# Gathers of half rows into both halves of the partitions, and down matrices laid out as 16 KB per partition

## The reference, cut to what matters

```python
    def expert_block(args):
        xb, e = args
        hmid = jax.nn.silu(xb @ w_gate[e]) * (xb @ w_up[e])   # (rows, 1024) x (1024, 512), twice
        return hmid @ w_down[e]                               # (rows, 512) x (512, 1024)
```

## Time and profile before

| | |
|---|---|
| median of 3 runs | 1599.68 us |
| the profiled execution | 1603.98 us |
| its span | 1601.9 us |
| PE busy | 1300.0 us (81%) |
| DVE / ACT / POOL busy | 395.9 / 202.2 / 205.9 us |
| mean granted TensorE clock | 0.943 of full |
| DMA traffic | 471.18 MB, mean 294 GB/s |

### The profile page before, as it was taken

How to read it: one execution, slowest core, us unless ns; L and a number is a source line. 1 busy time by engine, 2 the same in 40 slices (tenths; PEclk the granted TensorE clock), 3 DMA queues, 4 the chain that set the end, 5 groups by cost and what they waited for, 6 DMA issues and landing times.

```text
span 1601.9 us, 19565 instructions
## 1 busy us (share of the span) xinstructions
PE 1300.0 (81%) x8158; PEld 884.9 (55%) x8158; DVE 395.9 (25%) x809; ACT 202.2 (13%) x318; POOL 205.9 (13%) x228
## 2 busy tenths in 40 slices
PE   8999998999777787778369999799887787777850
PEld 7888876565444444444158887656444444444420
DVE  1211214431111111111145663443111111111116
ACT  1000011000000000000044652200000000000002
POOL 0000001122111111111010000112211111111104
PEclk8999998899999999999779999889999999999985
DMA  9922204799999999999793202469999999999954
GB/s 236 303 105 105 106 1 167 257 399 403 404 409 409 399 410 405 410 399 407 240 293 150 82 29 102 163 252 375 403 406 397 406 412 392 412 395 401 417 182 119
DMA packets 109162, 471.18 MB, mean 294 GB/s; under 512 B 14391, under 2 KB 49207, under 8 KB 91684
## 3 DMA queue, kind: packets, MB, share of 16 engines
q1 hardware_dynamic: 93324, 443.09, 72.2%
q0 software_dynamic: 10240, 17.06, 3.2%
q10 hardware_dynamic: 5552, 10.39, 2.3%
HBM read 459.53 MB, written 19.19 MB: 299 GB/s over the span
## 4 chain that ended last, share of the span: by engine, by line
PE 40%; DMA 29%; SPq 24%; DVE 3%; issue 2%; POOL 1%; ACT 1%; POOLq 0%; DVEq 0%; ACTq 0%
SPq L357 23%; PE ps L547 18%; DMA ring<-in_moe_w_gate 14%; PE ps L785 8%; PE ps L631 7%; DMA ring<-in_moe_w_up 6%; DMA ring<-in_moe_w_down 4%; PE ps L804 4%; DMA Bt<-yrows 1%; DMA ring<-yrows 1%; DMA ring<-in_a_w_in 1%; PE ps L775 1%; PE ps L649 1%; PE ps L683 1%; PE ps L571 1%
## 5 line engine op out<-in xcount | busy, mean ns | idle before, releaser
L785 PE MATMUL ps<-ring,A 128*64 128x256 f32 x4096 | 487.5, 393 | 144.7 <-DMA ring<-in_moe_w_up 97.2
L785 PEld LDWEIGHTS ps<-ring,A 128*64 128x64 f32 x4096 | 320.4, 142 | 332.8 <-issue 135.6
L547 PE MATMUL ps<-A,ring 128*128 128x260 f32 x1280 | 286.2, 386 | 2.5 <-DMA ring<-in_a_w_in 2.5
L804 PE MATMUL ps<-ring,C 128*64 128x512 f32 x1024 | 239.1, 609 | 40.1 <-DMA ring<-in_moe_w_down 15.8
L547 PEld LDWEIGHTS ps<-A,ring 128*128 128x128 f32 x1280 | 245.6, 192 | 41.0 <-issue 2.7
L1396 DVE TENSOR_TENSOR C<-C,ps 128x256 f32<-128x256 f32 x64 | 26.9, 420 | 769.9 <-ACT C L1017 769.9
L804 PEld LDWEIGHTS ps<-ring,C 128*64 128x64 f32 x1024 | 79.1, 139 | 159.3 <-issue 137.7
L484 POOL DMA_INDIRECT A<-x,idx x64 | 61.2, 957 | 487.1 <-PE ps L775 458.3
L631 PE MATMUL ps<-Bt,ring 128*128 128x260 f32 x512 | 116.1, 385 | 1.0 <-ACT C L942 0.8
L631 PEld LDWEIGHTS ps<-Bt,ring 128*128 128x128 f32 x512 | 96.1, 190 | 20.1 <-DVE A L1244 2.5
L1017 ACT ACTIVATE C<-ps 128x256 f32<-128x256 f32 x64 | 24.6, 384 | 569.3 <-PE ps L785 569.2
(11 more groups left out here) (210 smaller groups left out, 662.2 us busy)
## 6 DMA issues: line engine op xcount, KB each, us to landing
ring<-in_moe_w_gate SPq DMA_DIRECT2D x64, 2048.0 KB
ring<-in_moe_w_up SPq DMA_DIRECT2D x64, 2048.0 KB
ring<-in_moe_w_down SPq DMA_DIRECT2D x64, 2048.0 KB
ring<-in_a_w_in SPq DMA_DIRECT2D x24, 512.0 KB, 17.8
ring<-in_b_w_in SPq DMA_DIRECT2D x8, 1024.0 KB
ring<-yrows SPq DMA_DIRECT2D x8, 832.0 KB
x<-C ACTq DMA_DIRECT2D x10, 416.0 KB
ring<-in_a_w_out SPq DMA_DIRECT2D x2, 2048.0 KB
```

The costliest lines, as they stand in the source:

```text
L547: mm = pe.matmul(bank, lhs(k), rhs(k), start=(k == 0), stop=(k == KT - 1))
L785: mm = pe.matmul(ps[hf * ROWS:(hf + 1) * ROWS, 1, u * FH:(u + 1) * FH], xgT[:, k, :], ring[:, slot, col:col + FH], start=(k == 0), stop=(k ...
L804: mm = pe.matmul(ps[nh * ROWS:(nh + 1) * ROWS, 2, :], hidT[:, at:at + ROWS], ring[:, slot, m * D + nh * 512:m * D + (nh + 1) * 512], start ...
```

## The change

Four things are done.

1. The down matrices are laid out as `(p m)`: partition p holds rows 4p to 4p+3, one piece of 16 KB in DRAM. The DMA has the same bytes and the same destination slot.
2. `turn_hidden` has to give partition p the hidden values 4p to 4p+3. Two transposes become four pairs of 64 by 64 products with the identity (partitions 0 to 63 onto 0 to 63, and 64 to 127 onto 64 to 127), and one product of the whole identity with four of its columns stands ahead of them.
3. A token's row is gathered as two half rows of 2 KB by two indirect DMAs: the first half to partitions 0 to 47, the second half to partitions 64 to 111. `turn_rows` becomes eight pairs of 64 by 64 products. `xg` shrinks to half the width, and the numbers in `idx` are doubled, with one more table for the second half, in space of `A` that `xg` gave up.
4. The semaphores of the gathers count 32 instead of 16.

```diff
-        downs = [a["moe_w_down"][l].rearrange("e (m p) n -> e p m n", p=P) for l in L]
+        downs = [a["moe_w_down"][l].rearrange("e (p m) n -> e p (m n)", m=FT) for l in L]
...
-        xg = [A[:ROWS, i * D:(i + 1) * D] for i in range(UNROLL)]
+        xg = [A[:, i * 512:(i + 1) * 512] for i in range(UNROLL)]
+        idx = A[:CAP, UNROLL * 512:UNROLL * 512 + 2 * NBLK].bitcast(I32).rearrange("p (h b) -> p h b", h=2)
...
-                    out = ring[:, s, :] if u < 2 else ring[:, s, :].rearrange("p (m n) -> p m n", m=FT)
-                    sp.dma_start(out, w[l][e]).then_inc(loaded[s], 16)
+                    sp.dma_start(ring[:, s, :], w[l][e]).then_inc(loaded[s], 16)
...
+                def gather(rows, where, done):
+                    for h in range(2):
+                        pool.indirect_dma_start(
+                            out=rows[h * ROWS:h * ROWS + CAP, :], out_offset=None, in_=half_x1[l],
+                            in_offset=bass.IndirectOffsetOnAxis(ap=where(h), axis=0),
+                            bounds_check=2 * T - 1, oob_is_err=False,
+                        ).then_inc(done, 16)
...
                 def turn_rows(x, done, free=False):
                     xv = x.rearrange("r (p k) -> r k p", k=KT)
                     for k in range(KT):
-                        mm = pe.transpose(ps[:, 0, k * ROWS:(k + 1) * ROWS], xv[:, k, :], ident[:ROWS, :ROWS])
-                        if free and k == 0:
-                            mm.then_inc(freed, 1)
+                        for h in range(2):
+                            r = slice(h * ROWS, (h + 1) * ROWS)
+                            mm = pe.matmul(ps[r, 0, k * ROWS:(k + 1) * ROWS], xv[r, k, :], ident[r, r], start=True, stop=True)
+                            if free and k == 0 and h == 0:
+                                mm.then_inc(freed, 1)
...
                 def turn_hidden(done, free=False):
-                    for c in range(2):
-                        mm = pe.transpose(ps[:, 4, c * P:(c + 1) * P], gated[:, c * P:(c + 1) * P], ident[:, :])
-                        if free and c == 0:
-                            mm.then_inc(freed, 1)
+                    gv = gated.rearrange("r (p m) -> r m p", m=FT)
+                    pe.matmul(ps[:, 3, :4], ident[:, :], ident[:, :4], start=True, stop=True)
+                    for m in range(FT):
+                        for hf in range(2):
+                            r = slice(hf * ROWS, (hf + 1) * ROWS)
+                            mm = pe.matmul(ps[r, 4, m * ROWS:(m + 1) * ROWS], gv[r, m, :], ident[r, r], start=True, stop=True)
+                            if free and m == 0 and hf == 0:
+                                mm.then_inc(freed, 1)
...
                 def down(slot, done):
 
                     for m in range(FT):
-                        at = (m % 2) * P + (m // 2) * ROWS
                         for nh in range(2):
-                            mm = pe.matmul(ps[nh * ROWS:(nh + 1) * ROWS, 2, :], hidT[:, at:at + ROWS],
+                            mm = pe.matmul(ps[nh * ROWS:(nh + 1) * ROWS, 2, :], hidT[:, m * ROWS:(m + 1) * ROWS],
...
-                tsc(idx[:, :NE], ps[:CAP, 5, :NE], float(NOROW), ALU.add).then_inc(idx_ok[l], 1)
+                for h in range(2):
+                    ins = tsc(idx[:, h, :NE], ps[:CAP, 5, :NE], float(NOROW + h), ALU.add)
+                ins.then_inc(idx_ok[l], 1)
```

More of the change, by code:

```diff
@@ L118, in build @@
         rows_dram = nc.dram_tensor("yrows", [T, TOPK, D], F32).ap()
+        half_x1 = [x.rearrange("t (h n) -> (t h) n", h=2) for x in x1_dram]
         half_rows = rows_dram.rearrange("t k (h n) -> (t k h) n", h=2)
@@ L430, in _ @@
                         for u, w in enumerate((gates, ups, downs)):
-                            out = ring[:, u, :] if u < 2 else ring[:, u, :].rearrange("p (m n) -> p m n", m=FT)
-                            sp.dma_start(out, w[l][e]).then_inc(v_load[l], 16)
+                            sp.dma_start(ring[:, u, :], w[l][e]).then_inc(v_load[l], 16)
                     sp.wait_ge(over_done[l], 1)
@@ L499, in _ @@
                     if e < NE:
-                        gather(e)
+                        if e >= UNROLL:
+                            pool.wait_ge(t_mm[l], e - UNROLL + 1)
+                        gather(xg[e % UNROLL], lambda h: idx[:, h, e:e + 1], gath[UNROLL * l + e % UNROLL])
                     if e == UNROLL + 1:
@@ L516, in _ @@
                     with pool.Fori(0, n_over) as o:
-                        pool.tensor_copy(cur[:, 0:1], idx[:, bass.ds(o + NE, 1)]).then_inc(v_cur[l], 1)
-                        pool.tensor_copy(cur[:, 1:2], dest[:, 0, bass.ds(o + NE, 1)]).then_inc(v_cur[l], 1)
-                        pool.tensor_copy(cur[:, 2:3], dest[:, 1, bass.ds(o + NE, 1)]).then_inc(v_cur[l], 1)
-                        pool.wait_ge(v_cur[l], o * 5 + 3)
+                        for h in range(2):
+                            pool.tensor_copy(cur[:, h:h + 1], idx[:, h, bass.ds(o + NE, 1)]).then_inc(v_cur[l], 1)
+                            pool.tensor_copy(cur[:, 2 + h:3 + h], dest[:, h, bass.ds(o + NE, 1)]).then_inc(v_cur[l], 1)
+                        pool.wait_ge(v_cur[l], o * 6 + 4)
                         settle(0)
-                        pool.indirect_dma_start(
-                            out=xg[0][:CAP], out_offset=None, in_=x1_dram[l],
-                            in_offset=bass.IndirectOffsetOnAxis(ap=cur[:, 0:1], axis=0),
-                            bounds_check=T - 1, oob_is_err=False,
-                        ).then_inc(v_gath[l], 16)
+                        gather(xg[0], lambda h: cur[:, h:h + 1], v_gath[l])
                         pool.wait_ge(v_ya[l], o + 1)
                         settle(1)
-                        scatter(yo[0], lambda nh: cur[:, 1 + nh:2 + nh], v_out[l])
+                        scatter(yo[0], lambda nh: cur[:, 2 + nh:3 + nh], v_out[l])
                         pool.wait_ge(v_out[l], o * 32 + 32)
@@ L832, in _ @@
                 warm(WARM)
-                pe.wait_ge(gath[UNROLL * l], 16)
+                pe.wait_ge(gath[UNROLL * l], 32)
                 turn_rows(xg[0], t_mm[l])
```

19 lines of the change are left out of this document (5 added, 14 removed).

## The result

The changed kernel takes 1620.01 us, median of 4 runs (1616.84 to 1620.88); the kernel before took 1599.16 us beside it (1595.18 to 1599.91). The ratio is 1.0132, with an interval of 1.011 to 1.0154: slower by about 21 us, where 14 us of gain were forecast. It lies outside the range given.

What follows compares the result with a forecast made beforehand. The weight stream by DMA was taken as the bound, with PE hidden. Terms -31.9 + 5.8 + 10.2 + 1.6 = -14.3 us gave 1589.7 from the profiled 1603.98, shifted to the median: 1585.5 us predicted, range 1570 to 1608.

Steps and rivals of the forecast that it cites:

- Part 1: Weight stream: 16 KB instead of 4 KB pieces make down units arrive sooner, gaining 31.9 us (0 to 47).
- less 4.80 for the gate, the down unit took 5.61 us, 0.81 more for the same bytes: End of layer 1: 10.41 us from up to next gate, less one gate unit; the 0.81 was laid to 4 KB pieces.
- The 0.55 taken: Gain in us assumed for each down unit, between bounds of 0 and 0.81, counted for 58 units.
- Rival A: Weight stream: 4 KB pieces are no slower where it matters, gain 0 to 6 us, total 1614 us; chance 0.16.
- Part 2: Gathers in the stream: one more indirect DMA per expert costs 0.10 us, 5.8 us in all.
- Rival B: Gathers: an indirect DMA costs by number, 0.43 us each, 25 us instead of 5.8, total 1605 us; chance 0.13.
- Part 3: PE in the steady stretch: small products add 1.4 us an expert, hidden behind the weight stream, so no cost.
- against 3.9 of room before, 3.5 after: hidden: PE's spare us per expert mid-layer: stream period 16.44, then 15.99, less 12.52 of PE work; 1.4 extra fits.
- Rival C: PE becomes the bound: small products wait for one another at 277 ns, adding 5.3 us an expert, total 1695; chance 0.07.
- Part 4: Start of a layer: delays before the first down product hold back the stream, 5.1 us a layer, 10.2 for two.
- Part 5: End of a layer: `turn_hidden`'s extra 0.8 us shows in full, 1.6 us for two layers.
- What the views should have shown: PE timeline signs: middle period near 16.0 us; staying at 16.4 means A or B, no idling before up means C.

Runs made afterwards that it cites:

- two_gathers: Kernel before the change, with each gather as two half-row DMAs side by side on the same partitions, no small products: 1602.83 us, ratio 1.0029.
- down_turned: Kernel before, with down matrices in 16 KB pieces and gate and up columns reordered so two whole transposes still turn the hidden values: 1587.18 us, ratio 0.9928.
- filler_mid: Changed kernel plus four unused 128-column identity products per expert between `turn_rows` and `turn_hidden`: 1606.9 us, ratio 1.0065 to the kernel before.
- filler_wait: Changed kernel plus two unused 128-column identity products per expert between `turn_hidden` and the down product: 1610.66 us, ratio 1.008 to the kernel before.
- rows_small: One half of the change: kernel before with half-row gathers and new `turn_rows`, old down layout: 1612.66 us, ratio 1.0083.
- after_half: Changed kernel loading only half of each down matrix from the fourth expert on: 1619.38 us, ratio 1.0136 to the kernel before.
- down_small: Other half of the change: kernel before with new down layout and new `turn_hidden`, old gathers and `turn_rows`: 1595.03 us, ratio 0.9979.

## Why the prediction was wrong

**Part 1, the down matrices: the term mis-sized (forecast -31.9 us; measured -11.5).** The first failed step is "less 4.80 for the gate, the down unit took 5.61 us, 0.81 more for the same bytes". The subtraction gives the time in which a down and a gate unit arrive, with all that arrives or leaves beside them, and the data of two scatters fell there; nor were the DMA engines all busy (share 0.80 and 0.65). The same mistake had been seen for the middle of the layer ("traffic of gathers and scatters lies over it") and not at its end, where "gathers are over" was true but scatters weren't. The 0.55 taken was 0.2; of the 0.81, some 0.3 to 0.4 has no shown cause. Rival A, with the estimate of 0.1 us a unit from the Trainium skill ("DMA: Bandwidth & Descriptors", "Why small descriptors are slow (HBM only)"), was nearer on this term, though too low at 0 to 6 us. Its total of 1614 us lies near the measured 1620 by luck: it has PE hidden behind the stream, as my forecast had. The runs and the rule differ by about a factor of two: by the rule a 4 KB piece would lose 3 of 131 cycles, some 3.4 ns of the 4.8 / 32 = 0.15 us that it takes, as an estimate, and 8 ns were measured between 2 and 4 KB.

**Part 2, the gathers: right in the stretch, and too dear.** 0.10 us an expert was taken; `two_gathers` shows none, and 0.07 at most. Rival B, 0.43, falls with it. The cost of the second DMA is at the starts, 3 us each on average, where 1.3 and 0.15 had been counted.

**Part 3, PE in the steady stretch: the step that turned the sign.** The sizes were short but not far off: 1.4 us an expert forecast, 2.1 measured (14.62 against 12.52 for an expert that waits for nothing), half for each set of small products. Two things went wrong with "against 3.9 of room before, 3.5 after: hidden".
First, the room. It was the difference of two periods in the middle of the layer. But PE has to do 31 experts from the first down product to the last, and the stream only 29 of them, since the first ones lie in the ring. What counts is the stretch: `down_turned`'s 472.11 us, which the stream sets, less 31 x 12.52 = 388 us of PE, leaves 84 us, or 2.7 us an expert. This is also why the period in the middle could fall (16.44 us before, 15.7 after) while the stretch of layer 0 grew by 6 us: before, the first seven experts or so went by at 12.5 us each out of the full ring.
Second, the clock. With the small products the clock falls for the down product behind them: 19 slow ones a layer cost 31 us beyond 3.65 each, 1.0 us an expert. 2.1 alone would have been hidden (31 x 14.62 = 453 us, less than 472). 2.1 + 1.0 is not: 453 + 31 = 484 us, and 485.35 and 484.92 were measured. The fillers confirm both sides: `filler_mid` has 31 x 15.5 = 481 us, measured 481; `filler_wait` has 453 and some 3 us for three slow products, less than the stream's 472, and measures 475.39. So everything that the stream had gained in the stretches (472.11 against 479.33, 477.88 against 485.59, 15 us in all in these traces and 11.5 by the medians) was given back, and 5 us more. This is the main part of what the whole has beyond its halves: each half left PE below the stream, both together put it above. In the traces the stretches of the halves sum to -10.6 us, and those of the whole to +5.4.
Rival C named the place, PE becoming the bound, but by another mechanism, small products that wait for one another at 0.277 us. They ran two side by side, 16 in 2.14 us, 0.13 each, so a wait of each for the one before didn't show. "It decides from 3.5 us an expert on" should have read 2.7.

**Part 4, the starts: 5.1 us forecast, 8.4 and 7.5 measured.** The step that failed is the price of the delays before the first down product, in layer 1 above all. The rows that answer to the earlier trace rows:

```profile
275.22 5.49 PE L567 MATMUL ps<-ident 128*128 128x128 f32 x24
281.17 2.14 PE L773 MATMUL ps<-ident,A 64*64 64x64 f32 x32 [0.46 <-DMA A<-x,A]
...
287.26 8.87 PE L783 MATMUL ps<-ring,A 128*64 128x256 f32 x64 [3.95 <-DVE A L1396]
...
303.14 0.59 PE L792 MATMUL ps<-ident 128*128 128x4 f32 x2 [2.14 <-DVE C L1399]
...
305.45 4.85 PE L805 MATMUL ps<-ring,C 128*64 128x512 f32 x16 [0.57 <-issue]
```

The warm-up starts 275.22 - 274.48 = 0.7 later, but so do the products in front of it, which the change doesn't touch (over all the traces they start between 272.28 and 273.99 us). It isn't a cost of the second table of row numbers, for which 0.15 was forecast. The warm-up then takes 0.6 longer and ends into a wait of 0.46 for the gather: 1.1 together, 1.3 forecast. From `turn_rows` to the gate product it is 287.26 - 281.17 = 6.1 us, and was 2.7: 3.4 against the forecast 1.8. The record gives the sixteen small products 2.14 us and the granted clock is 1.00 over them, but DVE, which takes their result, starts only 4.6 us after the first of them, and 1.2 before:

```profile
285.79 0.69 DVE L1393 TENSOR_TENSOR A<-ps,gb 128x512 f32<-128x512 f32 x1 [6.38 <-remote]
```

The same holds in `rows_small`, `filler_wait` and `after_half` (4.6 to 4.7 us). But in `filler_mid`, whose program for PE is the same up to here, `turn_rows` starts at 279.53, DVE follows after 2.25 us, and the gate product after 3.7:

```profile
281.78 0.69 DVE L1395 TENSOR_TENSOR A<-ps,gb 128x512 f32<-128x512 f32 x1 [3.58 <-PE ps L773]
```

So the small products can be done in about 2.2 us at a layer's start too, and what holds their result back by 2.4 us in the other four kernels stays open. It is much of what `filler_mid` gained at the starts.

In layer 1 the second half's gather is waited for much longer, where nothing was waited for before (the turn of the rows followed the warm-up at 1040.91):

```profile
1046.10 1.81 PE L750 MATMUL ps<-Bt 104*48 104x32 f32 x20 [1.80 <-DVE Bt L1329]
1047.84 4.92 PE L567 MATMUL ps<-ident 128*128 128x128 f32 x24
1056.08 2.19 PE L773 MATMUL ps<-ident,A 64*64 64x64 f32 x32 [3.32 <-DMA A<-x,A]
```

Counted from the products that make the row numbers (L750 here, L754 before) to the first down product, a start took 24.3 and 23.7 us before. It is 1.5 and 5.5 us longer in `two_gathers`, 6.1 and 9.0 in `rows_small`, and 7.7 and 10.5 in the changed kernel. So the second gather, the small products for the rows and those for the hidden values (with all that came late behind them) cost 1.5, 4.6 and 1.6 us in layer 0 and 5.5, 3.5 and 1.5 in layer 1. The last is again a price of both together: in `down_small`, with the hidden products alone, a start takes 23.9 and 23.2 us, no longer than before.
The fourth expert's down matrix is issued 6.9 us later, forecast 5, and it moves the stream, as forecast (in `rows_small` the starts are longer and the stretches aren't shorter for it):

```profile
310.75 0.33 SPq L357 DMA_DIRECT2D ring<-in_moe_w_down  x1
```

**Part 5, the end of a layer.** The last expert (timeline of PE, answering to the earlier trace rows):

```profile
1563.22 0.39 PE L792 MATMUL ps<-ident 128*128 128x4 f32 x2 [0.93 <-DVE C L1399]
1563.53 1.17 PE L796 MATMUL ps<-ident,C 64*64 64x64 f32 x16
1565.28 3.65 PE L805 MATMUL ps<-ring,C 128*64 128x512 f32 x16 [0.57 <-issue]
```

From the start of `turn_hidden` to the down product it is 2.06 us instead of 1.00: 1.1, forecast 0.8. What I had no term for is the end of the run: from the last down product on it is 4.45 us shorter. `two_gathers` (54.37) and `rows_small` (54.15) have it too, `down_turned` (57.74) and `down_small` (59.67) don't. So it comes with the second gather. Most of it lies in POOL's last instruction, a drain at the end of its program (view of line L106, before and after):

```profile
L106 POOLq DRAIN  x1: 11612/11612/11612, 1590.1 to 1590.1; - x1
...
L106 POOLq DRAIN  x1: 4097/4097/4097, 1610.5 to 1610.5; - x1
```

Before, this drain ends at 1601.7 and is what the span ends on; after, it is over at 1614.6, and ACT, which issues the last stores, sets the end at about 1618.5. It takes 11.6 to 11.9 us in each of the six kernels with one gather for an expert, and 4.1 in each of the six with two. Why a drain gets shorter by it is open.

**What the views should have shown, and did.** The period in the middle was 15.7 us and PE no longer idled before up. The second was named as the sign of C, PE as the bound, and PE was. The first alone would have looked like a success.

Not tried: taking the product of the whole identity out of `turn_hidden`, so its share of the 1.1 us and of the clock's fall is open.

## What to carry to other kernels

Before moving work onto an engine that has "room", take the room over the whole stretch, with the head start that buffers give the other side, and add what the new work does to the granted clock of the large products behind it: here 2.1 us an expert would have been free, and 1.0 us of low clock made them dear. Where a layout needs the values in another order, look first for an order that an existing large operation can give for nothing: turning the columns inside the gate and up products got the long pieces and 11.5 us without a single small product. And before a difference of arrival times is laid to one cause, list the other transfers that are under way in it; an experiment that changes only that cause (here the piece's length) is cheap.

## What the runs showed of the hardware

- Pairs of 64 by 64 float32 products, on different halves of the partitions, run side by side: 16 in 2.14 us at the granted clock of 1.00, about 0.13 us each.
- Small products ahead of a large one can make the granted clock fall for it: 38 of 64 down products took 4.81 to 5.35 us instead of 3.65. With the small products for the rows alone (`rows_small`) none but the first of each layer was slow, with those for the hidden values alone (`down_small`) 15 more, with two large unused products put into the 0.57 us of idle time (`filler_wait`) 8 in all. Four large unused products in each expert (0.9 us) kept the clock at 1.00, and cost less than they saved.
- A moving operand read in pairs of columns with gaps costs a little: 3.84 us instead of 3.67 for 16 products of 256 columns.
- A DMA in shorter pieces is slower: from 4 to 2 KB a piece costs 8 ns on its engine beside its bytes; 16 KB pieces save 0.2 us of a unit of 2 MB against 4 KB ones.
- A second indirect DMA of half the bytes costs 0.07 us or less in a stretch that streams weights, and 1.5 and 5.5 us at the two starts where its result is waited for. The data of two scatters cost the stream 0.4 to 0.5 us an expert.
- A DMA share of 0.92 to 0.99 doesn't say that the stream is the bound: taking away a sixth of its bytes left the stretches as they were (`after_half`).
- POOL's drain at the end of its program took 11.6 us in the kernels with one gather for an expert and 4.1 in those with two.
